# FFN of a fused decoder layer: two sets of raw weights, weight sums on VectorE, late down products added straight from PSUM

## What is computed

```python
D_MODEL, SEQ, DEPTH, D_FF = 1024, 1024, 1, 2816
def swiglu(h, w_in, w_out):
    gate, up = jnp.split(h @ w_in, 2, axis=-1)
    return (jax.nn.silu(gate) * up) @ w_out
...
        h2 = rms_norm(x) * (1 + sc2) + sh2
        x = x + g2 * swiglu(h2, w_ffn_in[i], w_ffn_out[i])
```

## Time and profile before

| | us |
|---|---|
| Median of 3 runs (2894.0 to 2898.23) | 2897.82 |
| The profiled execution, its own time | 2898.26 |
| Its span in the trace | 2896.5 |
| Granted clock of TensorE over the span | 0.995 |

### The profile page before, as it was taken

How to read it: one execution, slowest core, us unless ns; L and a number is a source line. 1 busy time by engine, 2 the same in 40 slices (tenths; PEclk the granted TensorE clock), 3 DMA queues, 4 the chain that set the end, 5 groups by cost and what they waited for, 6 DMA issues and landing times.

```text
span 2896.5 us, 61004 instructions
## 1 busy us (share of the span) xinstructions
PE 2766.2 (96%) x25491; PEld 2291.9 (79%) x25491; DVE 1579.1 (55%) x1733; ACT 962.8 (33%) x1483; POOL 1021.1 (35%) x739
## 2 busy tenths in 40 slices
PE   5999999999999999999999999999999998999888
PEld 4797989888888888887877777888887777777667
DVE  5655454645464545587865665666476323325443
ACT  5312131213131212155556675111132323324333
POOL 1404040303031212143441112333334666766776
PEclk9999999999999999999999999999999999999999
DMA  6202020202010111133331212565221323235323
GB/s 215 63 21 68 12 76 11 69 18 62 25 55 25 55 32 38 63 111 118 114 102 35 61 47 85 194 212 178 70 58 30 98 81 95 89 90 171 124 87 92
DMA packets 255360, 235.00 MB, mean 81 GB/s; under 512 B 24353, under 2 KB 213883, under 8 KB 255099
## 3 DMA queue, kind: packets, MB, share of 16 engines
q1 hardware_dynamic: 241632, 183.74, 20.9%
q10 hardware_dynamic: 13467, 47.31, 4.6%
HBM read 184.08 MB, written 46.92 MB: 80 GB/s over the span
## 4 chain that ended last, share of the span: by engine, by line
PE 73%; POOL 12%; ACT 5%; issue 4%; DVE 3%; DMA 3%; SPq 0%; ACTq 0%; DVEq 0%; POOLq 0%
PE ps L306 49%; POOL w_lo L1003 7%; PE ps L1188 3%; PE ps L1202 3%; PE ps L1199 2%; PE ps L1166 2%; ACT w_hi L2157 2%; DMA w_raw<-in_w_ffn_in 1%; POOL arena L1026 1%; POOL arena L1022 1%; PE ps L1251 1%; POOL arena L1028 1%; POOL arena L1019 1%; PE ps L1388 1%; DMA w_raw<-in_w_ffn_out 1%
## 5 line engine op out<-in xcount | busy, mean ns | idle before, releaser
L306 PE MATMUL ps<-x_hi,w_hi 128*128 128x512 f32 (+1 forms) x2372 | 805.2, 399 | 26.9 <-ACT arena L2202 9.8
L306 PE MATMUL ps<-x_lo,w_hi 128*128 128x512 f32 (+1 forms) x2372 | 785.0, 391 | 0.0
L306 PE MATMUL ps<-x_hi,w_lo 128*128 128x512 f32 (+1 forms) x2372 | 784.9, 391 | 0.0
L296 POOL CAST w_hi<-w_raw 128x1024 fp32r<-128x1024 f32 (+2 forms) x161 | 151.9, 943 | 1543.0 <-PE ps L306 1286.9
L306 PEld LDWEIGHTS ps<-x_hi,w_hi 128*128 128x128 f32 (+1 forms) x2372 | 438.0, 188 | 142.9 <-issue 31.9
L306 PEld LDWEIGHTS ps<-x_hi,w_lo 128*128 128x128 f32 (+1 forms) x2372 | 445.1, 188 | 97.0
L306 PEld LDWEIGHTS ps<-x_lo,w_hi 128*128 128x128 f32 (+1 forms) x2372 | 445.6, 188 | 92.3
L298 POOL TENSOR_TENSOR w_lo<-w_raw,w_hi 128x1024 fp32r<-128x1024 f32 (+2 forms) x161 | 330.1, 2050 | 12.9
L306 PE MATMUL ps<-x_sums,w_hi 128*128 128x512 f32 x648 | 208.0, 403 | 35.8 <-ACT arena L2202 35.5
L1003 POOL TENSOR_TENSOR w_lo<-arena,w_hi 128x512 fp32r<-128x512 f32 (+1 forms) x124 | 163.4, 1327 | 87.7 <-ACT w_hi L2157 87.7
L2157 ACT ACTIVATE w_hi<-arena 128x512 fp32r<-128x512 f32 (+1 forms) x124 | 72.0, 586 | 342.0 <-POOL arena L1022 160.1
(11 more groups left out here) (333 smaller groups left out, 4297.0 us busy)
## 6 DMA issues: line engine op xcount, KB each, us to landing
w_raw<-in_w_in SPq DMA_DIRECT2D x78, 512.0 KB, 3.9
arena<-in_w_ada SPq DMA_DIRECT2D x48, 512.0 KB, 6.0
w_raw<-in_w_ffn_in SPq DMA_DIRECT2D x44, 512.0 KB, 4.0
arena<-gates_sig ACTq DMA_DIRECT2D x40, 512.0 KB, 4.3
gates_sig<-arena ACTq DMA_DIRECT2D x24, 512.0 KB, 2.7
hidden_sums<-arena SPq DMA_DIRECT2D x36, 256.0 KB, 2.6
w_raw<-in_w_ffn_out SPq DMA_DIRECT2D x48, 192.0 KB, 2.8
under<-hidden_sums SPq DMA_DIRECT2D x11, 768.0 KB, 5.0
```

The costliest lines, as they stand in the source:

```text
L296: nc.gpsimd.tensor_copy(hi, raw).then_inc(s_whi, 1)
L306: ins = nc.tensor.matmul(dst[h], wp, xp[h], start=first and m == 0, stop=last and m == 2, skip_group_check=on)
```

## The change

- A second set of raw weights: items alternate between two sets (`raw_set`), and SP loads item n when the low parts of item n-2 are done, an item ahead. The second set lies in memory beside the stage sums, which now have one set of stages where there were two (`t2_stage` ...).
- POOL makes low parts alone. DVE makes the weight sums (`weight_sum`): in an up tile S4 of the present item first, and S1, S2, S3 of the next after the first add from PSUM; in a late pair those of the next pair, one after each of the products 1 to 4 (in the first pair of a span, two after 5 and two after 6).
- Late pairs: no copies by ACT and no sums of banks. DVE adds each of the seven products from PSUM to `x2` (some twice-used results are written so that every product has one target), and PE waits for those adds.
- Operands of the next span get their low parts in thirds (`operand_low_third`), spread by a table over the slots between the adds; ACT's high parts move too.
- The wait conditions of loads, stores and output follow.

```diff
-        s_fw = [counted_on(s_lw, PAIRS * 96), counted_on(s_mask, 16)]
         s_st = [counted_on(s, 16 * (b - a_)) for s, (a_, b) in zip(s_ada[:4], ADA_PARTS)]
+        s_fw = [[counted_on(s_lw, PAIRS * 96), counted_on(s_mask, 16)], [counted_on(s_x2, 128), s_st[3]]]
...
-        MADE_IN = {}
+
+        HIGH_IN, LOW_IN = {}, {}
+            for o, high, *low in ((O_B11, (1, 4), (1, 6), (1, 6), (2, 0)), (O_B21, (1, 5), (2, 0), (2, 1), (2, 2)),
+                                  (O_T2, (2, 4), (2, 6), (3, 0), (3, 0)), (O_T1, (3, 3), (3, 5), (3, 5), (3, 6)),
...
+        N_LAST = ITEMS.index(("down", DOWNS - 1))
+
+        def raw_set(n):
+
+            return n % 2 if n > N_LAST else 1 - n % 2 if 1 < n < N_LAST else 0
+
+        def raw_parts(n):
+
+            if raw_set(n) == 0:
+                return raw_a, raw_b
+            return under_hid[:, 1024:2048], under_hid[:, 3072:4096]
+
+        def raw_quarters(n):
+
+            if n > N_LAST and raw_set(n) == 1:
+                return [raw_place(k)[:, 0:WIDTH["late"]] for k in (24, 25, 19, 6)]
+            return [raw[:, c][:, 0:WIDTH[ITEMS[n][0]]] for raw in raw_parts(n) for c in COLS]
+
+
+        def weight_sums(n):
+
+            if ITEMS[n][0] == "late":
+                return [t[:, 0:WIDTH["late"]] for t in (sum_a, sum_b, raw_place(26), raw_place(14))]
+            return [sum_a, sum_b, raw_place(14) if n == 1 else under_hid[:, 2560:3072], sum_b]
...
+        def add_done(i, j):
+
+            return 3 * FAST + 7 * i + j + 1
 
         def weights_loaded(n):
 
-            return 16 * sum(LOADS[kind] for kind, _ in ITEMS[:n + 1])
+            return 16 * sum(LOADS[kind] for m, (kind, _) in enumerate(ITEMS[:n + 1]) if raw_set(m) == raw_set(n))
+
+        def wait_weights(eng, n, part):
+
+            loaded = s_fw[raw_set(n)][part]
+            eng.wait_ge(loaded, begun[loaded.num] + weights_loaded(n))
...
+                for part in range(2):
+                    if n == 0:
+                        sp.wait_ge(s_wsplit, upto(Block("ffn", 2 + part).before + 1))
+                    elif n == 1:
+                        sp.wait_ge(f_lo, late(f_lo, PIECE0[ITEMS[0]] + 2 * part + 2))
+                    elif n == N_LAST and part == 0:
+                        sp.wait_ge(f_lo, late(f_lo, PIECE0[ITEMS[n - 1]] + PC_A12 + 1))
+                        sp.wait_ge(f_s, late(f_s, sums_before(n)))
+                    elif n == N_LAST:
+                        sp.wait_ge(f_lo, late(f_lo, PIECE0[ITEMS[n]]))
+                    else:
+                        sp.wait_ge(f_lo, late(f_lo, PIECE0[ITEMS[n - 1]]))
+                        if n == 2:
+                            sp.wait_ge(f_used, late(f_used, PIECE0["down", 0] + 4))
+                        elif n == N_LAST + 1:
+                            sp.wait_ge(f_h, late(f_h, 2 * FAST))
+                    load_weights(n, part)
+                    if n == N_LAST:
+                        for o in ((O_B11, O_B21, O_T2), (O_T1, O_B22, O_T4))[part]:
+                            load_operand(0, o)
                 if kind == "up" and i % 2 == 1 and i >= 5:
                     store_sums((i - 5) // 2)
...
-                    elif part == 0:
-                        sp.wait_ge(f_s, late(f_s, sums_before(n)))
-                    else:
-                        sp.wait_ge(f_lo, late(f_lo, PIECE0[ITEMS[n]]))
...
+                elif kind == "late" and i == SPANS * M_PAIRS - 1:
+                    for j in range(4 * (M_PAIRS - 2)):
+                        store_out(j)
...
-                piece_low(item, PC_A11)
-                pool.wait_ge(s_fw[1], begun[s_fw[1].num] + weights_loaded(n))
-                if s0 > 0:
-                    pool.wait_ge(f_lo, late(f_lo, PIECE0[item]))
-                gp.tensor_tensor(sa, a21, a22, ALU.add).then_inc(f_s, 1)
-                piece_low(item, PC_A12)
-                pool.wait_ge(f_s, late(f_s, s0 + 1))
-                gp.tensor_tensor(sb_, sa, a11, ALU.subtract).then_inc(f_s, 1)
-                piece_low(item, PC_S2)
-                piece_low(item, PC_S1)
-                pool.wait_ge(f_lo, late(f_lo, PIECE0[item] + PC_S1 + 1))
-                gp.tensor_tensor(sa, a11, a21, ALU.subtract).then_inc(f_s, 1)
-                piece_low(item, PC_S3)
-                gp.tensor_tensor(sb_, a12, sb_, ALU.subtract).then_inc(f_s, 1)
-                piece_low(item, PC_S4)
-                piece_low(item, PC_A22)
+            for item in ITEMS:
+                for j in range(PIECES[item[0]]):
+                    piece_low(item, j)
...
-                pe.wait_ge(f_h, late(f_h, 2 * (q - 2) + 1))
+                if n < 2:
+                    pe.wait_ge(f_h, late(f_h, 2 * FAST))
+                else:
+                    pe.wait_ge(f_post, late(f_post, add_done(n - 2, 6)))
                 product(0, b1, True)
                 if out_pair is not None and out_pair > 0:
                     out_quarter(4 * out_pair - 1)
-                pe.wait_ge(f_post, late(f_post, 3 * (q - 1) + 1))
+                if n > 0:
+                    pe.wait_ge(f_post, late(f_post, add_done(n - 1, 1)))
                 product(1, d, True)
-                pe.wait_ge(f_snap, late(f_snap, 3 * q + 1))
+                pe.wait_ge(f_post, late(f_post, add_done(n, 0)))
                 product(2, b1, False)
-                pe.wait_ge(f_post, late(f_post, 3 * (q - 1) + 3))
+                if n > 0:
+                    pe.wait_ge(f_post, late(f_post, add_done(n - 1, 5)))
                 product(3, c, True)
-                pe.wait_ge(f_snap, late(f_snap, 3 * q + 2))
+                pe.wait_ge(f_post, late(f_post, add_done(n, 2)))
                 product(4, b1, False)
                 if out_pair is not None:
                     out_quarter(4 * out_pair)
-                pe.wait_ge(f_snap, late(f_snap, 3 * q + 3))
+                pe.wait_ge(f_post, late(f_post, add_done(n, 3)))
                 product(5, c, False)
-                pe.wait_ge(f_post, late(f_post, 3 * q + 2))
+                pe.wait_ge(f_post, late(f_post, add_done(n, 4)))
                 product(6, b1, False)
...
-                        if j in (0, 2, 3):
-                            snap(FAST + i, r0, j)
                         piece_high(r0 + j + QUARTERS)
-                        for n in MADE_IN.get((i, j), ()):
+                        for n in HIGH_IN.get((i, j), ()):
                             operand_high(n)
...
+            def weight_sum(n, which):
+
+                a11, a12, a21, a22 = raw_quarters(n)
+                s1, s2, s3, s4 = weight_sums(n)
+                s0, r0 = sums_before(n), PIECE0[ITEMS[n]]
+                before = next((PIECE0[item] for item in reversed(ITEMS[:n]) if item[0] != "down"), None)
+
+                def split_before(j):
+
+                    if before is not None:
+                        dve.wait_ge(f_lo, late(f_lo, before + j + 1))
+                if which == 1:
+                    wait_weights(dve, n, 1)
+                    split_before(PC_S1)
+                    ins = v.tensor_tensor(s1, a21, a22, ALU.add)
+                elif which == 2:
+                    wait_weights(dve, n, 0)
+                    split_before(PC_S2 if ITEMS[n][0] == "late" and n > N_LAST + 1 else PC_S4)
+                    dve.wait_ge(f_s, late(f_s, s0 + 1))
+                    ins = v.tensor_tensor(s2, s1, a11, ALU.subtract)
+                elif which == 3:
+                    split_before(PC_S3)
+                    if n == 1:
+                        dve.wait_ge(c_lo, late(c_lo, ALL_SUMS))
+                    elif n == 2:
+                        dve.wait_ge(f_used, late(f_used, PIECE0["down", 0] + 4))
+                    elif n == N_LAST + 1:
+                        dve.wait_ge(f_h, late(f_h, 2 * FAST))
+                    ins = v.tensor_tensor(s3, a11, a21, ALU.subtract)
+                else:
+                    if ITEMS[n][0] == "up":
+                        dve.wait_ge(f_lo, late(f_lo, r0 + PC_S2 + 1))
+                    elif n == N_LAST + 1:
+                        dve.wait_ge(m_hl, upto(4))
+                    else:
+                        split_before(PC_S4)
+                    dve.wait_ge(f_s, late(f_s, s0 + 2))
+                    ins = v.tensor_tensor(s4, a12, s2, ALU.subtract)
+                ins.then_inc(f_s, 1)
 
             def operand_low(n):
...
+            def operand_low_third(n, k):
+
+                hi, lo, raw = (next(ap[:, k - k0, :] for ap, k0 in reversed(parts) if k0 <= k) for parts in operand_place(n))
+                if k == 0:
+                    dve.wait_ge(c_hi, late(c_hi, ALL_SUMS + n + 1))
+                ins = v.tensor_tensor(lo, raw, hi.bitcast(F32), ALU.subtract)
+                if k == HALF_SPAN - 1:
+                    ins.then_inc(c_lo, 1)
+
             def fast_hidden(tile):
+                weight_sum(n, 4)
                 if tile % 2 == 0:
                     stage_sums(pair)
                 dve.wait_ge(f_used, late(f_used, r0 + 2))
```

(33 more changed lines are left out.)

142 lines of the change are left out of this document (51 added, 91 removed).

## The result

The changed kernel takes 2813.94 us (median of 4 runs, 2812.41 to 2816.26) against 2896.34 us of the kernel before on the same chip (2894.0 to 2898.23). The ratio is 0.9717, 95% interval 0.970 to 0.9733. The forecast was 2831 us with a range of 2818 to 2852: both gains came, and the one of the late pairs was larger than I had it, by more than the range allowed.

A forecast was written before the change was run, and what follows sets the result against it. PE was taken to bound the kernel, stopping in up tiles and late pairs through a loop of POOL's sums, ACT's parts and raw-weight loads. 2898.26 less 44.1 (up tiles) and 22.9 (late pairs) gave 2831 us, range 2818 to 2852.

The forecast's parts named there:

- Where PE stopped and why: Up tiles and late pairs: PE waits for ACT's copies, held up by POOL's sums and late raw weights; excess 46.1 and 38.9 us.
- Loads an item ahead, margin 9 us: Up tiles: loads land some 16 us into the tile, first used at 25 us, so the raw-weight wait goes.
- Sums in the up tiles: Up tiles, sums moved from POOL to DVE: tiles run at PE's pace, excess 46.1 becomes 2, gain 44.1 us.
- the leftover 16: Late pairs: stops and lower-clock time that remain of 38.9 us of excess, leaving a gain of 22.9 us.
- My table: Late pairs 4 and 8: timeline of DVE's adds and nine thirds, making PE stop 3.3 us each, 6.6 in all.
- Pair 0 (1.6): Late pair 0: the first item's four sums make DVE reach the add that product 2 waits for 1.6 us late.
- Pairs 2 and 6 (2): Late pairs 2 and 6: thirds beside sums make adds 2 and 3 late, 1 us each pair, 2 in all.
- DVE and POOL hold each other up: SBUF operations: the two share a locked port pair; by this rule pair 4 stops 1.3 us.
- DVE as the new bound of the late pairs: Rival, late pairs: DVE and POOL take turns, thirds and sums cost 1.5 us, no gain there; 2854 us, chance 0.15.
- A stop left in the up tiles: Rival, up tiles: second add of even tiles late, 2.2 us in 9 tiles, or S4 late; 2851 us, chance 0.08.
- The change not doing what it says: Rival: PE did not wait for the copies, load or high part is next; one 22 us gain goes; 2875, chance 0.03.
- Slower by raw weights that land too late: Rival, up tiles: raw weights land after DVE's S1 wants them, 3.9 us a tile lost; 2905 us, chance 0.02.

The follow-up runs named there:

- sums on GpSimd: The changed kernel with all weight sums made by GpSimd again at their old places; second set and adds from PSUM stay: 2825.5 us.
- one-set kernel with the sums later: The changed kernel with one raw-weight set in the up tiles and VectorE's first three sums of the next tile behind the add of product 5: 2814.1 us.
- second set alone: The changed kernel with sums back on GpSimd and copies back in the late pairs; only the second set and earlier loads stay: 2833.3 us.
- the set with the sums on VectorE: The changed kernel with ScalarE's copies out of PSUM back in the late pairs; second set and VectorE's sums stay: 2821.0 us.
- three thirds more: The changed kernel with one spare 128x512 subtraction in each of the first three slots of late pairs 4 and 8: 2819.6 us.
- thin low parts: The changed kernel with GpSimd making only 32 of the 384 columns of each low part in the late pairs: 2814.7 us.
- one-set kernel with the sums ahead of the add: The changed kernel with one raw-weight set in the up tiles, VectorE's sums still before the add of product 4: 2872.8 us.
- sums by VectorE alone: The kernel before with only VectorE's weight sums and the operands' thirds; one raw-weight set, late pairs copying from PSUM: 2859.6 us.

## Why the prediction was wrong

**Where PE stopped and why: right, but too narrow.** ACT's waits for POOL's sums and for raw weights were the cause, and they vanished. I took the loads an item ahead as what cures the up tiles. They do it alone (sums on GpSimd), but the one-set kernel with the sums later shows that the sums on VectorE do it alone as well.

**Loads an item ahead, margin 9 us: right.** ACT waits for raw weights once, 1.0 us. In the up tiles the loads into the second set land in 5.3 us, not 4:

```profile
under<-in_w_ffn_in SPq DMA_DIRECT2D x18, 512.0 KB, 5.3
```

**Sums in the up tiles: right.** Gain 47.2 for 44.1 us. The 2 us that I left for the edges were not there; S4 took 1.64 to 1.80 us on average, near the high end, the first three sums 0.68 to 1.19, and the tile had room for both. This term is 3 of the 17 us by which the forecast was too high.

**The late pairs: the mechanism right, the leftover 16 mis-sized by 14 us.** This step failed, and it is what put the time below the range. The prediction also books the late gain under the adds from PSUM, which is not where it came from: of the 37.5 us from the last down product on, the second set alone gives 20.8, the set with the sums on VectorE 35.3, and the adds from PSUM the last 2.2. Stops of over 0.1 us are 1.6 us in the twelve pairs and 0.5 us in the last down product. PE stops at products 5 and 6 of pair 4 and in pair 8, where the prediction said, for 0.92 and 0.53 us in place of 3.3 each. DVE in pair 4 (which starts at 2681.65), changed kernel:

```profile
2683.99 0.75 DVE L3027 SCALAR_TENSOR_TENSOR arena<-ps,mod,arena 128x512 f32<-128x512 f32 x1
2684.66 2.04 DVE L2982 TENSOR_TENSOR x_lo<-under,x_hi 128x512 fp32r<-128x512 f32 x2
2686.62 0.74 DVE L3027 SCALAR_TENSOR_TENSOR arena<-ps,mod,arena 128x512 f32<-128x512 f32 x1
...
2691.41 1.44 DVE L2982 TENSOR_TENSOR x_sums<-arena,x_sums 128x512 fp32r<-128x512 f32 x2
2692.77 0.74 DVE L3027 SCALAR_TENSOR_TENSOR arena<-ps,mod,arena 128x512 f32<-128x512 f32 x1
2693.43 1.46 DVE L2982 TENSOR_TENSOR x_sums<-arena,x_sums 128x512 fp32r<-128x512 f32 x2
```

My table had the last two thirds ready 15.5 us into the pair; they are at 13.2 (2694.89). Of the 2.3 us, 0.4 are an earlier first add; 1.5 are the thirds, which cost 0.9 to 1.0 each where they begin beside a fresh low part of GpSimd and 0.7 in the last two slots; some 0.35 are the adds, which take 0.75 each but start 0.66 us before what follows them. A chain 2.3 us shorter makes 3.3 into 1.0, against 0.92 measured, and the three thirds more brought 2.0 of it back. (The prediction's own entries, 15.5 us where 6 x 2.06 = 12.4 was wanted, give 3.1 and not 3.3 us, so the table by itself leads to 0.8.) GpSimd in the same stretch:

```profile
2684.52 1.02 POOL L1052 TENSOR_TENSOR w_lo<-arena,w_hi 128x384 fp32r<-128x384 f32 x1 [1.05 <-ACT w_hi L2186]
...
2690.69 1.01 POOL L1052 TENSOR_TENSOR w_lo<-w_raw,w_hi 128x384 fp32r<-128x384 f32 x1 [1.01 <-ACT w_hi L2186]
2692.73 1.01 POOL L1052 TENSOR_TENSOR w_lo<-w_raw,w_hi 128x384 fp32r<-128x384 f32 x1 [1.03 <-ACT w_hi L2186]
```

At 2684.66 the thirds begin while a low part has 0.9 us to go, and wait for it; at 2691.41 and 2693.43 the low part began with the add from PSUM and has 0.3 us left. The average of the thirds was right, and the average was not what the critical slots pay.

The other terms of the 16 came out at nothing. Pair 0 (1.6): the four sums of the first item ran with GpSimd idle, 0.55 us each:

```profile
2619.32 0.55 DVE L2944 TENSOR_TENSOR arena<-arena 128x384 f32<-128x384 f32 x1
...
2620.48 0.55 DVE L2958 TENSOR_TENSOR arena<-arena 128x384 f32<-128x384 f32 x1
2620.95 0.55 DVE L2967 TENSOR_TENSOR arena<-arena 128x384 f32<-128x384 f32 x1
```

Pairs 2 and 6 (2): in pair 2 the adds 2 and 3 end 7.6 and 9.7 us into the pair, where I had 8.5 and 11.1 and 8.2 and 10.6 were wanted. Pairs 1, 5 and 9 (1.5), the third span (1.5) and the lower clock (3) have no stop at all, and a clock of 1.00. Most were allowances for a lateness that the slack of 1 us in a slot absorbs, since VectorE catches up in the next slot, and I had added them up as if each reached TensorE; the 1.5 us of the third span had no row behind it, and the 3 us at the lower clock rested on stops that did not come. In the prediction itself stood the sum at 0.69 us throughout, 6 us left, as the range's low end; with 1.6 us left even that was too much.

**DVE and POOL hold each other up: right.** The Trainium skill ("SBUF — State Buffer", Terms) has the two take turns for whole instructions. The kernel with thin low parts agrees: 1006 to 707 ns and 1370 to 592. The prediction's estimate by that rule, 1.3 us in pair 4, came nearer to the 0.92 measured than my 3.3, but by luck: it lays the work of both engines end to end over the pair, puts in four sums that are made behind products 5 and 6, and leaves out DVE's adds. The stops come from the order in which the thirds are wanted, with POOL idle half of the time.

**The rivals.** DVE as the new bound of the late pairs: no, it is idle for 33 us of the 182. A stop left in the up tiles: none. The change not doing what it says: no, both gains came, though its premise that PE didn't wait for the copies as such holds in the late pairs; its price was also mixed up, for without the 22 us of the late pairs 2854 would result, and 2875 only without the 44 of the up tiles. Slower by raw weights that land too late: not here, but it is what happened in the one-set kernel with the sums ahead of the add, where PE waited 34.0 us, and in nine late pairs of the kernel with sums by VectorE alone, 27.7 us.

## What to carry to other kernels

When a loop through several engines and a load is longer than the step it feeds, ask which member to take out before doubling a buffer: here moving four operations off GpSimd, at the right place in VectorE's list, was worth as much in the up tiles as moving them and doubling the buffer. Where an in-order engine takes over work that waits for a load, put it behind the operation that TensorE waits for. And a lateness counts only once it exceeds the slack that is left at that place: carry one timeline through the slots, with the durations of those slots, instead of adding an allowance for each. Last, read in the trace where a moved operation really stands before taking a difference of two kernels as the price of one part.

## What the runs showed of the hardware

VectorE's operations from SBUF took 0.55 us (128x384) and 0.69 us (128x512) with GpSimd idle, and 1.37 and 1.80 us when they began just beside a GpSimd operation; reads from PSUM stayed at 0.75 us in both kernels. I had not expected the price to depend on the moment so much: two thirds cost 2.04 us when they start 0.14 us after the start of a low part and 1.44 us when they start 0.7 us after it. Which of the two engines waits goes by which began first. In the changed kernel from 2237 us on, all 109 VectorE operations of 128x512 with both inputs in SBUF that began with GpSimd idle took 0.68 to 0.69 us, also the 59 during which a GpSimd operation began, and the 40 that began with over 0.8 us of one to go took 1.36 to 1.80. GpSimd's own low parts of 128x512 took 1.28 to 1.31 us when they began beside no VectorE operation, and 1.37 to 2.54 when they began within one from SBUF. The same 128x384 low part by GpSimd, 1.14 us on average before, took 1.04 us in the changed kernel. VectorE's operations in a row start 0.08 us before the recorded end of the one ahead, so a sum of their lengths is too long by some 10%.
